# Sums of squares of the difference heads: two split passes with a low part from GpSimd, in place of one full-precision sum

## The chip, the cores and the metric

One core of a Trainium2 chip runs the whole program, a single launch. The metric is device time in microseconds (us) from one execution to the next of the same program, and a shorter time is better. Three runs of the kernel before are known, and one further execution that the hardware profiler recorded.

## What is computed

The program is a chain of two models on 512 tokens of width 1024, all in float32: one block with two kinds of attention, then four layers, each a mixer and a gated feed-forward network with a short convolution. The mixer is difference attention in layers 0 and 3, stick-breaking attention in layer 1 and sliding-window attention in layer 2. The change touches difference attention alone, and there only the norm of a head's output:

```python
def rmsnorm(x, g):
    xf = x.astype(jnp.float32)
    y = xf * lax.rsqrt(jnp.mean(xf * xf, axis=-1, keepdims=True) + EPS)
    return (y * g.astype(jnp.float32)).astype(x.dtype)

def diff_attention(h, w_qkv, lam, subln, rel_bias, lambda_init):
    ...
    def block(args):
        ...
        p = jax.nn.softmax(s, axis=-1)
        a = p[:, :, 0] - lam_full * p[:, :, 1]
        return jnp.einsum('bhqk,bkhe->bqhe', a.astype(v.dtype), v)

    o = lax.map(block, (q_blocks, jnp.arange(nb) * BLOCK))
    o = jnp.moveaxis(o, 0, 1).reshape(B, S, DA_HEADS, DA_V_DIM)
    o = rmsnorm(o, subln) * (1.0 - lambda_init)
    return o.reshape(B, S, DA_HEADS * DA_V_DIM)
```

There are 8 heads of 128 values each, and the mean of squares runs over the 128 values of a head, for each of the 512 tokens.

## The kernel before, in words

Each engine has a program of its own, written out by hand, and semaphores tie them together. A head's output lies with its 128 values on the partitions and the 512 tokens along the row, so a sum over the values is a product with a 128x128 matrix of ones, which also spreads the sum to all partitions.

**Products of the weights.** Weights come from memory in pieces of 128x2048. To multiply float32 data in single passes, each operand is split in two parts of the type fp32r: `whi` is the rounded weight (ScalarE, `split_hi`, L1162), `wlo` is the rest (GpSimd, four instructions of 512 columns a piece, L1113), and `three_passes` (L462) adds hi*hi, hi*lo and lo*hi. The data are split in the same way into `xh` and `xl`. Most of the kernel's TensorE time is spent in that one line.

**The mixer.** In `mix_diff` of TensorE (L909) the heads are staggered. Turn t of the loop works on head t: scores (L883), then their transposition (`turn`, L888). In the same turn it finishes head t-1: `pv` (L927) multiplies the weights of attention with the values, and `squares` (L933) sums the squares of the result, into the same PSUM bank `out`. Between these steps it fills in quanta of other work, the projections of later heads and, toward the end, the first part of the output product: `work.fill(n)` issues n quanta, `work.fill_to(n)` issues until n are done. A quantum is three passes of 512 columns where q and k are made, and six passes of 256 columns where v is made. `STARTS` says how many quanta must be done when a turn's scores begin, and three lines in the loop matter here:

```python
            work.fill(4 if last else 6)
            if t >= 1:
                squares(t - 1)
            work.fill_to(starts[t] + 20 if last else starts[t + 1] - 2)
            turn(t)
```

**What the other engines do in turn t.** VectorE (`mix_diff`, L1986) takes the scores from PSUM, adds the bias and their minimum (L2003), takes a projected unit, then copies the output of head t-1 to `od` (L2014), makes the low part of head t-2 (`ol`, L2018), the reciprocals (L2022, L2024), scales the second softmax (four instructions, `e1_scaled`, L2028), takes a projected unit (L1968), and combines the two softmaxes (four instructions, `normed`, L2033), which `turn` of TensorE waits for one by one. Then it reads the sum of squares of head t-1 (`ov`, L2040), waits for ScalarE's logarithm and exponential of it (L1452, L1454), scales the head (L2043), and takes the unit 3t+4 (L1968 for q and k, L1962 for v). Units 7, 13 and 19 are the k of heads 2, 4 and 6, and the scores of these heads wait for them.

ScalarE (`mix_diff`, L1419) copies the turned weights (`aT`, L1431), splits the head (L1435), takes the exponentials (L1416), squares `od` of head t-1 into `sq` (L1447), and then waits for `ov`. The table `HI_AT` says at which of three places of a turn it makes the high part of which piece: before the copy (place 0), after the exponentials (place 1) or after the square (place 2). In turns 1, 3 and 5 a piece stands at place 2, in turns 2, 4 and 6 one stands at place 1. GpSimd (`pool_program`) makes the low part of each piece as soon as its high part is there.

`var` is a buffer of the layer norms, which is free while a mixer runs.

## Time and profile before

| | |
|---|---|
| time, median of 3 runs | 2717.31 us (2715.97 to 2717.72) |
| time of the profiled execution | 2716.34 us |
| span of the profiled execution, first to last instruction | 2714.5 us |
| mean granted TensorE clock, share of full speed | 0.993 |
| TensorE (PE) busy | 2658.9 us, 98% of the span |
| TensorE weight loads (PEld) busy | 2129.7 us, 78% |
| VectorE (DVE) busy | 1460.9 us, 54% |
| GpSimd (POOL) busy | 1158.2 us, 43% |
| ScalarE (ACT) busy | 1117.7 us, 41% |

The difference between the profiled execution's time and its span, 1.8 us, lies before the first and after the last instruction. Busy shares are averages over the whole program. The first difference mixer lies at about 381 to 592 us of the span, the second at about 2111 to 2322 us. In the rows of the trace a matmul's own duration is longer than its share of the engine, since matmuls overlap in the array: the distance from one start to the next says what one costs. In the same way an instruction of VectorE is recorded from some 0.08 us before the one ahead of it ends.

### The profile page before, as it was taken

Reading aid. Unit: us, or ns where it says so; the run is one execution under the profiler, and the core shown is the slowest. Engines: PE = TensorE matmul, PEld = TensorE weight load, DVE = VectorE, ACT = ScalarE, POOL = GpSimd, SP = SyncE. Lnnn points to the kernel's source line nnn. Section 1 sums busy time; section 2 is a strip of 40 time slices with the busy share of each in tenths; the row PEclk is TensorE's granted clock in tenths of the full one; section 3 lists DMA queues with packets and bytes.
Section 4 is the critical chain, followed back from the end, with each engine's and each line's share of the span. In section 5 each row is a group of like instructions: output and inputs, shape, how many; then the busy total and the mean of one; then the engine's idle time right before and its main releaser. Section 6 shows DMA issues by size and latency. Waiting matters only on the chain.

```text
span 2714.5 us, 32020 instructions
## 1 busy us (share of the span) xinstructions
PE 2658.9 (98%) x12868; PEld 2129.7 (78%) x12868; DVE 1460.9 (54%) x2608; ACT 1117.7 (41%) x1509; POOL 1158.2 (43%) x876
## 2 busy tenths in 40 slices
PE   8998999999999999999999999999999999999997
PEld 7786687778888877778888886888888777888886
DVE  5797555557554135657554145575522565565522
ACT  4534644444333236654333236443333344443331
POOL 3353343235445532335444542254455332454452
PEclk9899999999999999999999999999999999999999
DMA  4125032222223221112223331222233222222332
GB/s 163 63 96 184 1 117 86 78 78 93 93 97 110 104 97 63 63 63 93 94 93 110 108 124 48 78 93 94 99 110 117 94 86 70 94 93 93 106 112 78
DMA packets 45605, 253.44 MB, mean 93 GB/s; under 512 B 4560, under 2 KB 9184, under 8 KB 17936
## 3 DMA queue, kind: packets, MB, share of 16 engines
q1 hardware_dynamic: 34656, 232.18, 24.4%
q10 hardware_dynamic: 10800, 19.20, 2.1%
q8 instruction: 102, 1.67, 0.2%
q14 instruction: 47, 0.39, 0.0%
HBM read 249.21 MB, written 10.55 MB: 96 GB/s over the span
## 4 chain that ended last, share of the span: by engine, by line
PE 92%; DVE 4%; ACT 2%; POOL 1%; issue 1%; DMA 0%; DVEq 0%; SPq 0%; ACTq 0%
PE ring L462 78%; PE ring L883 3%; PE turn L888 2%; PE turn L462 1%; PE out L927 1%; POOL wlo L1113 1%; PE ring L720 1%; PE ring L621 1%; PE out L736 1%; DVE sp L2065 1%; PE out L933 0%; DVE e L2033 0%; ACT whi L1162 0%; PE out L1015 0%; DVE z L2068 0%
## 5 line engine op out<-in xcount | busy, mean ns | idle before, releaser
L1113 POOL TENSOR_TENSOR wlo<-raw,whi 128x512 fp32r<-128x512 f32 x840 | 1124.0, 1369 | 1476.7 <-ACT whi L1162 1476.7
L462 PE MATMUL ring<-xh,whi 128*128 128x512 f32 x1888 | 753.2, 399 | 12.2 <-DVE xl L1616 8.5
L462 PE MATMUL ring<-xh,wlo 128*128 128x512 f32 x1888 | 736.8, 390 | 0.0
L462 PE MATMUL ring<-xl,whi 128*128 128x512 f32 x1888 | 736.3, 390 | 0.0
L1162 ACT ACTIVATE whi<-raw 128x2048 fp32r<-128x2048 f32 x215 | 411.2, 1913 | 432.7 <-DMA raw<-in_pieces 418.0
L462 PEld LDWEIGHTS ring<-xh,whi 128*128 128x128 f32 x1888 | 355.0, 188 | 117.5 <-issue 44.2
L462 PEld LDWEIGHTS ring<-xh,wlo 128*128 128x128 f32 x1888 | 354.9, 188 | 74.8
L462 PEld LDWEIGHTS ring<-xl,whi 128*128 128x128 f32 x1888 | 355.2, 188 | 72.4 <-issue 3.4
L2181 DVE SCALAR_TENSOR_TENSOR taps<-u,conv,taps 128x511 f32<-128x511 f32 (+1 forms) x344 | 296.9, 908 | 17.7 <-ACT taps L1558 15.7
L2195 DVE TENSOR_TENSOR u<-ring,r 128x512 f32<-128x512 f32 x168 | 114.3, 686 | 298.5 <-PE ring L462 298.5
L2169 DVE TENSOR_TENSOR h<-ring,h 128x512 f32<-128x512 f32 x72 | 49.5, 689 | 418.4 <-PE ring L809 376.1
L1558 ACT ACTIVATE taps<-u,conv 128x512 f32<-128x512 f32 x172 | 137.9, 808 | 303.5 <-DVE u L2195 303.5
L462 PE MATMUL ring<-hh,wlo 128*128 128x512 f32 x672 | 261.6, 389 | 0.0
L462 PE MATMUL ring<-hl,whi 128*128 128x512 f32 x672 | 261.6, 389 | 0.0
L462 PE MATMUL ring<-hh,whi 128*128 128x512 f32 x672 | 261.6, 389 | 0.0
L462 PE MATMUL ring<-whi,xh 128*128 128x256 f32 (+1 forms) x576 | 181.7, 315 | 0.7 <-POOL wlo L1113 0.7
L462 PE MATMUL ring<-wlo,xh 128*128 128x256 f32 (+1 forms) x576 | 173.8, 302 | 0.0
L462 PE MATMUL ring<-whi,xl 128*128 128x256 f32 (+1 forms) x576 | 173.6, 301 | 0.0
L462 PEld LDWEIGHTS ring<-hl,whi 128*128 128x128 f32 x672 | 126.2, 188 | 26.1
L462 PEld LDWEIGHTS ring<-hh,wlo 128*128 128x128 f32 x672 | 126.2, 188 | 26.1
L462 PEld LDWEIGHTS ring<-hh,whi 128*128 128x128 f32 x672 | 126.2, 188 | 26.1
L1561 ACT ACTIVATE taps<-taps 128x512 f32<-128x512 f32 x88 | 55.7, 633 | 173.7 <-DVE taps L2181 173.7
(282 smaller groups left out, 3410.9 us busy)
## 6 DMA issues: line engine op xcount, KB each, us to landing
raw<-in_pieces SPq DMA_DIRECT2D x215, 1024.0 KB, 4.7
toep<-diag_store ACTq DMA_DIRECT2D x16, 512.0 KB, 3.6
diag_store<-diag_row ACTq DMA_DIRECT2D x1, 5120.0 KB, 26.0
band_store<-band_row ACTq DMA_DIRECT2D x1, 3072.0 KB, 33.0
h<-in_x SPq DMA_DIRECT2D x4, 512.0 KB, 6.7
wbias<-band_store ACTq DMA_DIRECT2D x4, 512.0 KB, 7.3
result<-h SPq DMA_DIRECT2D x8, 256.0 KB, 2.1
raw<-in_pieces SPq DMA_DIRECT2D x4, 256.0 KB, 6.9
```

Source lines behind the costliest of these rows:

```text
L462: ins = pe.matmul(out, stationary, moving, start=first and n == 0, stop=last and n == 2)
L621: ins = pe.matmul(out, x[:, tok], weights[slot][:, w], start=i == 0 and weights is m.whi and x is passes[0][0], stop=i == len(tiles) - 1 a ...
L720: pe.matmul(bank(("score", p, j, i))[:, 0:n], q[:, i * P:(i + 1) * P], k[:, 0:n], start=True, stop=True).then_inc(m["unit_ready"], 1)
L883: pe.matmul(m.ring[2 + j][:, 0:n], qs[part, i * P:(i + 1) * P], ks[part, lo:lo + n], start=True, stop=True).then_inc(m["su_ready"], 1)
L888: ins = pe.transpose(m.turn[:, to:to + P], src[:, at:at + P], m.ident[:])
L1113: ins = pool.tensor_tensor(m.wlo[slot][:, part], m.raw[slot][:, part], m.whi[slot][:, part].bitcast(F32), ALU.subtract)
L1162: act.activation(m.whi[p % SLOTS][:], m.raw[p % SLOTS][:], ACT.Copy).then_inc(m["hi_done"], 1)
L1558: act.activation(taps[g][:], m.u[g][:], ACT.Identity, scale=cols[:, 4 * g + 2:4 * g + 3], bias=cols[:, 4 * g + 3:4 * g + 4]).then_inc(m["t ...
L1561: act.activation(taps[0][0:rows, :], taps[0][0:rows, :], ACT.Silu).then_inc(m["silu"], 1)
L2169: dve.tensor_tensor(m.h[:, k, :], ring(b, k)[:], m.h[:, k, :], ALU.add).then_inc(m["unit_taken"], 1)
L2181: dve.scalar_tensor_tensor(y[:, shift:S], m.u[g][:, 0:S - shift], cols[:, tap:tap + 1], y[:, shift:S], ALU.mult, ALU.add).then_inc(m[signa ...
L2195: dve.tensor_tensor(m.u[g][:], ring(b, 2 * t + g)[:], m.r[:], ALU.mult).then_inc(m["unit_taken"], 1)
```

## The change

For heads 0 to 6 of both difference mixers the sum of squares is taken in two passes over fp32r operands. ScalarE squares `od` twice: once in float32 into `sq`, as before, and once more, rounded to fp32r, into `osq_h` (in the place of `var`). GpSimd subtracts the one from the other and writes the rest as `osq_l` into the place of `sq`. TensorE multiplies both parts with `ones_r`, a copy of the ones as fp32r, and adds the two in PSUM. The last head of a mixer is summed as before. In TensorE's loop the sum stands four quanta later. GpSimd makes a head's low part after the low part of the last piece whose high part ScalarE makes ahead of that head's square. VectorE makes `ones_r` once, in the first stage.

```diff
--- before.py
+++ after.py
@@ -188,7 +188,7 @@
         heads = TILES if mixer == "diff" else 2 * TILES
         t.update({"turned": heads, "at_ready": heads})
         if mixer == "diff":
-            t.update(exped=64, rl_ready=8, c1_ready=8, e1_scaled=32, normed=32, o_taken=8, osq_ready=8, osum_done=8,
+            t.update(exped=64, rl_ready=8, c1_ready=8, e1_scaled=32, normed=32, o_taken=8, osq_ready=8, osqh_ready=7, osql_ready=7, osum_done=8,
                      ov_ready=8, oln_ready=8, ors_ready=8, on_ready=8)
         elif mixer == "stick":
             t.update(absed=16, expabs=16, lned=16, above_ready=16, scanned=64, arg_ready=16)
@@ -293,6 +293,7 @@
         self.cols = self.keep("cols", [P, N_COLS])
         self.ident = self.keep("ident", [P, P])
         self.ones = self.keep("ones", [P, P])
+        self.ones_r = self.keep("ones_r", [P, P], F32R)
         self.r = self.keep("r", [P, S])
         self.var = self.keep("var", [P, S])
         self.rtok = self.keep("rtok", [P, TT])
@@ -310,6 +311,9 @@
         sq_at = end - 4096
         self.sq = self.at("sq", [P, 2, S], sq_at)
         self.y = self.at("y", [P, S], sq_at)
+
+        self.osq_h = self.at("osq_h", [P, S], self.place["var"], F32R)
+        self.osq_l = self.at("osq_l", [P, 2, S], sq_at, F32R)
 
 
         consts = base + 49152
@@ -929,8 +933,15 @@
             ins.then_inc(m["pv_done"], 1)
 
         def squares(h):
-            pe.wait_ge(m["osq_ready"], b.at("osq_ready", h + 1))
-            pe.matmul(m.out[:], m.ones[:], m.sq[:, h % 2, :], start=True, stop=True).then_inc(m["osum_done"], 1)
+            if h == TILES - 1:
+                pe.wait_ge(m["osq_ready"], b.at("osq_ready", h + 1))
+                pe.matmul(m.out[:], m.ones[:], m.sq[:, h % 2, :], start=True, stop=True).then_inc(m["osum_done"], 1)
+                return
+
+            pe.wait_ge(m["osqh_ready"], b.at("osqh_ready", h + 1))
+            pe.matmul(m.out[:], m.ones_r[:], m.osq_h[:], start=True, stop=False)
+            pe.wait_ge(m["osql_ready"], b.at("osql_ready", h + 1))
+            pe.matmul(m.out[:], m.ones_r[:], m.osq_l[:, h % 2, :], start=False, stop=True).then_inc(m["osum_done"], 1)
         for t in range(TILES):
             work.fill_to(starts[t])
             pe.wait_ge(m["pu_taken"], b.at("pu_taken", K_UNIT[t] + 1))
@@ -943,7 +954,7 @@
                 work.fill(2)
             if t >= 1:
                 pv(t - 1)
-            work.fill(4 if last else 6)
+            work.fill(8 if last else 10)
             if t >= 1:
                 squares(t - 1)
             work.fill_to(starts[t] + 20 if last else starts[t + 1] - 2)
@@ -1099,12 +1110,27 @@
         for i in range(TT):
             row = m.e_1[p % 2][1][:, BLOCK_OFF[i]:BLOCK_OFF[i] + CAUSAL_W[i]]
             pool.tensor_scalar(row, row, m.rl[:, p % 2, 1, i:i + 1], None, ALU.mult).then_inc(m["normed_1"], 1)
+    def square_low(mb, h):
+
+
+        pool.wait_ge(m["osq_ready"], mb.at("osq_ready", h + 1))
+        pool.wait_ge(m["osqh_ready"], mb.at("osqh_ready", h + 1))
+        pool.tensor_tensor(m.osq_l[:, h % 2, :], m.sq[:, h % 2, :], m.osq_h[:].bitcast(F32),
+                           ALU.subtract).then_inc(m["osql_ready"], 1)
+
+    heads = {}
+    for name in st:
+        if name.startswith("mix") and MIXER[int(name[3:])] == "diff":
+            for h in range(TILES - 1):
+                last = max(j for j, where in HI_AT["diff"].items() if where <= (h + 1, 1))
+                heads.setdefault(st[name].at("piece", last), []).append((st[name], h))
     for p in range(1, n_pieces):
 
         if p == b.at("piece", 3):
             for pair in range(PAIRS):
                 normalise(pair)
         if p in by_vector:
+            assert p not in heads
             continue
         slot = p % SLOTS
         pool.wait_ge(m["hi_done"], p)
@@ -1113,6 +1139,8 @@
             ins = pool.tensor_tensor(m.wlo[slot][:, part], m.raw[slot][:, part], m.whi[slot][:, part].bitcast(F32),
                                      ALU.subtract)
         ins.then_inc(m["lo_done"], 1)
+        for mb, h in heads.get(p, ()):
+            square_low(mb, h)
 
 
 def sync_program(sp, m, d, ends, finish):
@@ -1445,6 +1473,10 @@
                 if h >= 2:
                     act.wait_ge(m["osum_done"], b.at("osum_done", h - 1))
                 act.activation(m.sq[:, h % 2, :], m.od[h % 3][:], ACT.Square).then_inc(m["osq_ready"], 1)
+                if h < TILES - 1:
+                    if h >= 1:
+                        act.wait_ge(m["osum_done"], b.at("osum_done", h))
+                    act.activation(m.osq_h[:], m.od[h % 3][:], ACT.Square).then_inc(m["osqh_ready"], 1)
             hi_at(b, "diff", t, 2)
             if 1 <= t < TILES + 1:
                 h = t - 1
@@ -1632,7 +1664,8 @@
         dve.wait_ge(m["unit_ready"], b.at("unit_ready", k + 1))
 
     def first(b):
-        dve.memset(m.ones[:], 1.0).then_inc(m["set_up"], 1)
+        chain(dve.memset(m.ones[:], 1.0))
+        dve.tensor_copy(m.ones_r[:], m.ones[:]).then_inc(m["set_up"], 1)
         for k in range(KT):
             if k % 2 == 0:
                 part = slice(256 * k, 256 * k + 512)
```

What moves can be seen in the order of the instructions. On TensorE, at the sum of head 0 in turn 1 (`xh` and `xl` are the data, `whi` and `wlo` the weights; the numbers in names count the buffers of the program). Before:

```order
L462 MATMUL ring<-xh,wlo_59 128x512
L933 MATMUL out<-sq,ones 128x512
L462 MATMUL ring<-xh,whi_56 128x512
L462 MATMUL ring<-xl,whi_56 128x512
L462 MATMUL ring<-xh,wlo_59 128x512
```

With the change:

```order
L466 MATMUL ring<-xh,whi_57 128x512
L466 MATMUL ring<-xl,whi_57 128x512
L466 MATMUL ring<-xh,wlo_60 128x512
L942 MATMUL out<-osq_h,ones_r 128x512
L944 MATMUL out<-osq_l,ones_r 128x512
L466 MATMUL ring<-xh,whi_57 128x512
```

The one sum has become two products, and they stand 12 matmuls later (row 1586 of TensorE's order, before row 1574), already among the matmuls of the next piece of weights. Where the quanta are those of v, as in turns 2, 4 and 6, four of them are 24 matmuls of 256 columns.

On GpSimd, from the low part of piece 4 to that of piece 7 (`wlo` is written over `raw`). Before:

```order
L1113 TENSOR_TENSOR wlo_60<-raw_54,whi_57 128x512 x4
L1113 TENSOR_TENSOR wlo_58<-raw_52,whi_55 128x512 x4
L1113 TENSOR_TENSOR wlo_59<-raw_53,whi_56 128x512 x4
L1113 TENSOR_TENSOR wlo_60<-raw_54,whi_57 128x512 x4
L1113 TENSOR_TENSOR wlo_58<-raw_52,whi_55 128x512 x4
```

With the change:

```order
L1139 TENSOR_TENSOR wlo_60<-raw_54,whi_57 128x512 x4
L1118 TENSOR_TENSOR osq_l<-sq,osq_h 128x512
L1139 TENSOR_TENSOR wlo_58<-raw_52,whi_55 128x512 x4
L1139 TENSOR_TENSOR wlo_59<-raw_53,whi_56 128x512 x4
L1118 TENSOR_TENSOR osq_l<-sq,osq_h 128x512
L1139 TENSOR_TENSOR wlo_60<-raw_54,whi_57 128x512 x4
L1118 TENSOR_TENSOR osq_l<-sq,osq_h 128x512
L1139 TENSOR_TENSOR wlo_58<-raw_52,whi_55 128x512 x4
```

The first `osq_l` is of head 0 (turn 1), and the low part of piece 5 now stands behind it. The second, of head 1 (turn 2), follows straight upon piece 6. The third is of head 2 (turn 3).

On ScalarE, behind the exponentials of turn 1. Before:

```order
L1403 DMA toep_190<-diag_store 128x2x512
L1447 ACTIVATE sq<-od_193 128x512
L1162 ACTIVATE whi_55<-raw_52 128x2048
L1452 ACTIVATE ov_191<-ov_191 128x512
L1454 ACTIVATE ov_191<-ov_191 128x512
```

With the change:

```order
L1431 DMA toep_193<-diag_store 128x2x512
L1475 ACTIVATE sq<-od_196 128x512
L1479 ACTIVATE osq_h<-od_196 128x512
L1190 ACTIVATE whi_55<-raw_52 128x2048
L1484 ACTIVATE ov_194<-ov_194 128x512
L1486 ACTIVATE ov_194<-ov_194 128x512
```

The second square stands ahead of the high part of piece 5.

## Rows read from the trace of the kernel before

**Rows 1.** The page's busy times, and the chain that ended last, by engine.
```profile
PE 2658.9 (98%) x12868; PEld 2129.7 (78%) x12868; DVE 1460.9 (54%) x2608; ACT 1117.7 (41%) x1509; POOL 1158.2 (43%) x876
...
PE 92%; DVE 4%; ACT 2%; POOL 1%; issue 1%; DMA 0%; DVEq 0%; SPq 0%; ACTq 0%
```
**Rows 2.** Timeline of PE, turns 1 and 4: start, length in us, engine, line, operation.
```profile
429.49 0.39 PE L462 MATMUL ring<-xl,whi 128*128 128x512 f32 x1
429.71 0.39 PE L462 MATMUL ring<-xh,wlo 128*128 128x512 f32 x1
...
432.52 0.49 PE L883 MATMUL ring<-kt,qt 64*128 64x128 f32 x4
...
496.44 0.28 PE L462 MATMUL ring<-whi,xl 128*128 128x256 f32 x1
496.56 1.02 PE L933 MATMUL out<-sq,ones 128*128 128x512 f32 x2
...
497.54 0.28 PE L462 MATMUL ring<-wlo,xh 128*128 128x256 f32 x1
```
**Rows 3.** Timeline of PE where turns 2, 3, 5 and 6 end.
```profile
454.34 0.36 PE L462 MATMUL ring<-whi,xh 128*128 128x256 f32 x1
...
481.07 0.49 PE L883 MATMUL ring<-kt,qt 64*128 64x128 f32 x4 [0.50 <-DVE kt L1968]
...
531.04 0.49 PE L883 MATMUL ring<-kt,qt 64*128 64x128 f32 x4
...
551.01 1.51 PE L888 MATMUL turn<-ident,e 128*128 128x128 f32 x10
552.28 0.37 PE L462 MATMUL ring<-whi,xh 128*128 128x256 f32 x1
```
**Rows 4.** Timeline of DVE, turn 2, and the last of L2033 in turn 6.
```profile
447.56 3.29 DVE L2028 TENSOR_SCALAR e<-e,c 128x128 f32<-128x128 f32 x4
450.77 0.68 DVE L1968 SCALAR_TENSOR_TENSOR kt<-ring,r 128x512 f32<-128x512 f32 x1
451.37 1.93 DVE L2033 SCALAR_TENSOR_TENSOR e<-e,rl,e 128x128 f32<-128x128 f32 x4
...
549.89 1.92 DVE L2033 SCALAR_TENSOR_TENSOR e<-e,rl,e 128x128 f32<-128x128 f32 x4
```
**Rows 5.** Timeline of DVE, turn 3, and where turn 5 ends.
```profile
470.03 1.28 DVE L2028 TENSOR_SCALAR e<-e,c 128x128 f32<-128x128 f32 x4
471.82 5.87 DVE L2033 SCALAR_TENSOR_TENSOR e<-e,rl,e 128x128 f32<-128x128 f32 x4
...
480.33 0.68 DVE L1968 SCALAR_TENSOR_TENSOR kt<-ring,r 128x512 f32<-128x512 f32 x1
...
530.18 0.68 DVE L1968 SCALAR_TENSOR_TENSOR kt<-ring,r 128x512 f32<-128x512 f32 x1
```
**Rows 6.** Timeline of POOL, turns 1 to 4.
```profile
423.61 6.04 POOL L1113 TENSOR_TENSOR wlo<-raw,whi 128x512 fp32r<-128x512 f32 x4 [14.20 <-ACT whi L1162]
...
444.49 5.48 POOL L1113 TENSOR_TENSOR wlo<-raw,whi 128x512 fp32r<-128x512 f32 x4 [14.84 <-ACT whi L1162]
...
471.58 5.57 POOL L1113 TENSOR_TENSOR wlo<-raw,whi 128x512 fp32r<-128x512 f32 x4 [9.46 <-ACT whi L1162]
...
493.01 5.48 POOL L1113 TENSOR_TENSOR wlo<-raw,whi 128x512 fp32r<-128x512 f32 x4 [15.86 <-ACT whi L1162]
```
**Rows 7.** Timeline of ACT, turns 1 and 3.
```profile
421.10 0.63 ACT L1447 ACTIVATE sq<-od 128x512 f32<-128x512 f32 x1 [2.96 <-DVE od L2014]
421.63 1.90 ACT L1162 ACTIVATE whi<-raw 128x2048 fp32r<-128x2048 f32 x1
...
478.33 0.63 ACT L1452 ACTIVATE ov<-ov 128x512 f32<-128x512 f32 x1 [6.83 <-DVE ov L2040]
```
**Rows 8.** Timeline of DVE, turn 1.
```profile
421.47 1.28 DVE L2028 TENSOR_SCALAR e<-e,c 128x128 f32<-128x128 f32 x4
423.27 3.99 DVE L2033 SCALAR_TENSOR_TENSOR e<-e,rl,e 128x128 f32<-128x128 f32 x4
```

## The prediction, made before the change was run

> **What bounds the kernel now.** I read the page first. TensorE is busy for 98% of the span and holds 92% of the chain that ended last [rows 1], so time that leaves TensorE shows in the total, unless another engine takes it back, and time that another engine gains or loses counts only where TensorE waits for it. Those places had to be found in the timelines, because inside the two difference mixers TensorE has little slack beside VectorE. Rows 3 show three such places a mixer. In turn 3 the scores of head 4 wait 0.50 us for `kt`. In turn 5 the scores of head 6 start at 531.04, right behind the `kt` of rows 5, which ends at 530.18 + 0.68 = 530.86. In turn 6 the transposition takes 1.27 us to the next matmul (551.01 to 552.28): it waits in its middle for the last `normed`. So I had to price the change on both engines.
>
> **The gain on TensorE.** In turn 4 the last narrow pass before the sum starts at 496.44, the second behind it at 497.54 [rows 2]. Two narrow steps of 0.12 us would take 0.24 of that, so the sum costs 1.10 - 0.24 = 0.86 us. (Its recorded 1.02 us contains overlap.) The two passes that replace it have the form of L462's, of 512 columns, two of which start 0.22 us apart, at 429.49 and 429.71 [rows 2]; other pairs of them lie 0.23 apart, the rows being rounded. I take 0.23 each, 0.46 for both. That is 0.40 us less per head, and 14 heads give 5.6 us if nothing else moves. Making `ones_r` in the first stage is one short operation of VectorE while the first data are still on their way, so it costs nothing (0.7 us if that cover were gone, by a 512-column operation of VectorE [rows 4]).
>
> **ScalarE.** A second square costs one more step of 0.53 us, the distance from `sq` to the next instruction [rows 7]. ScalarE then waits for `ov` anyway (6.83 us idle in turn 3 [rows 7]), which hides it. Not hidden is that the high part of a piece, where one follows the square (turns 1, 3, 5), comes 0.53 us later, and GpSimd's low part with it.
>
> **GpSimd, and what it does to VectorE.** This is the term that decides. GpSimd's new instruction has the size of one of its four per piece: 5.48 us for four, two of which VectorE stretches [rows 6], so near 1.3 us each. Rows 4 and 5 show what such an instruction does to VectorE where VectorE reads and writes SBUF alone. The four L2028 take 1.28 us in turn 3, with GpSimd idle, and 3.29 us in turn 2, with two of GpSimd's instructions beside them: 1.0 us for each. The four L2033 take 1.93 us in turn 2 and 5.87 us in turn 3, beside four: again 1.0 us for each. The two take turns, instruction by instruction. `qt` and `kt`, which read PSUM, take 0.68 us either way. I take 1.0 us for a hit; the bounds are 0 (GpSimd's instruction meets only PSUM readers) and 1.3 us (all of it).
>
> The Trainium skill, page "SBUF — State Buffer", section "Who interferes with whom", says that the pair of ports shared by VectorE and GpSimd is an exclusive lock, held for a whole instruction, and that the loser blocks fully. By that a hit could cost all of GpSimd's instruction, 1.3 us in place of 1.0, and the sum below would be 1.2 us higher. The rows show 1.0, since VectorE's own time partly overlaps the wait, and I stay with them.
>
> **Turn by turn**, with the shift of TensorE against before at the start of the next scores (negative is earlier). All numbers are of mixer 0; mixer 3 repeats its rows.
>
> - Turn 1 (head 0). GpSimd's low part can start when the second square ends: 421.63 + 0.63, and 0.08 to wake (as from 421.63 + 1.90 to 423.61 [rows 6, 7]), 422.34. The four L2028 end at 422.75 [rows 8], and the fourth, of 512 columns, takes somewhat under 0.5 us, so it starts near 422.27. I take VectorE to be first. Then GpSimd starts at 422.75, L2033 loses some 0.5 us, and ends at 427.8 in place of 423.27 + 3.99 = 427.26 [rows 8]. The scores of head 2 (432.52) have room for that, so the shift is -0.40.
> - Turn 2 (head 1). GpSimd goes on from 444.49 + 5.48 = 449.97 [rows 6] straight into the low part and hits the third L2028 (+1.0). `normed` ends at 453.30 [rows 4] - 0.40 + 1.0 = 453.90. In turn 6 the next matmul comes 0.47 us after the last `normed` (549.89 + 1.92 = 551.81 [rows 4], then 552.28 [rows 3]), so here at 454.37, against 454.34 [rows 3]. Shift +0.03: the gain is lost.
> - Turn 3 (head 2). The low part hits L2028 (+1.0), but L2033 starts inside GpSimd's work on the piece in any case, and its end is set by that, which is 0.53 later. `kt` ends at 481.01 [rows 5] + 0.03 + 0.53 = 481.57, the scores start 0.06 later at 481.63 against 481.07. Shift +0.56.
> - Turn 4 (head 3). VectorE loses 1.0 but is early enough. TensorE comes to the second pass at 496.56 + 24 * 0.12 + 0.23 = 499.67; the low part is there at 493.01 + 5.48 + 1.28 + 0.08 = 499.85 [rows 2, 6]. A wait of 0.18, and some 0.1 to start again. Shift +0.56 - 0.40 + 0.3 = +0.46.
> - Turn 5 (head 4). As turn 3, `kt` ends at 530.86 + 0.46 + 0.53 = 531.85, scores at 531.91 against 531.04. Shift +0.87.
> - Turn 6 (head 5). The transposition already waits for `normed`, which is another 1.0 later. Shift +1.87.
> - Turn 7 (head 6). VectorE has room; TensorE keeps its 0.40. Shift +1.47.
>
> So each mixer ends 1.5 us later, and the two together 2.9 us. Against the profiled execution's own 2716.34 us that is 2719.2 us. It lies 1.0 us below the median of the runs, so the forecast is 2717.31 + 2.9 = 2720.2 us: 0.1% slower, which a measurement of this kernel can hardly tell from no change (about 0.2%, 5.4 us, is what it can tell).
>
> **Rival 1, slower: GpSimd is first in turn 1.** The two starts in turn 1 lie 0.07 us apart, and no row settles who wins such a meeting. If GpSimd gets in before the fourth L2028, that instruction ends near 423.8, `qt` near 424.4, and by then GpSimd has begun the piece (423.61 + 0.53 = 424.14). L2033 then runs as in turn 3, 5.87 us from 424.3 to 430.2, not to 427.26. From there to the end of `kt` turn 3 needs 481.01 - 477.69 = 3.3 us [rows 5], so `kt` is ready at 433.5, and the scores of head 2 start 1.0 us late, not 0.4 early. That is 1.45 us a mixer on top of everything above: +5.8 us, 2723.1 us. For it speaks that the gap is so small; against it that VectorE's instruction is recorded first. The page named above says, in the same section, that whoever starts first has the lock for the whole instruction. By the recorded starts this favours my forecast, and by the real end of the instruction ahead (0.08 us later than the record) it favours this rival.
>
> **Rival 2, faster: the collisions fall into slack.** If the low part meets only PSUM readers or idle time and nothing else is late, TensorE still cannot be earlier at the scores of head 4 or in the transposition of turn 6, since `kt` and `normed` wait for VectorE there. The gain of turns 3 and 6 is lost, and of turn 5 about 0.3. What stays is near 0.40 * 4 + 0.1 = 1.7 us a mixer: -3.4 us, 2713.9 us. Against it speaks that in turns 2, 4 and 6 GpSimd's fifth instruction follows the fourth without a pause, beside VectorE's L2028.
>
> **Rival 3, the whole gain.** If the waits of rows 3 shift along with the scores that begin their turn and VectorE is never the limit, all 5.6 us arrive: 2711.7 us. The 0.50 us wait in rows 3 speaks against it.
>
> **How the numbers follow.** I give the forecast 0.45, with another 0.07 for a course between it and rival 2, rival 1 0.28, rival 2 0.12, rival 3 with whatever else would make it faster 0.08. The range has to reach rival 2 on one side and rival 1 with a full price of hits (+1.2 us) on the other: 2713.2 to 2724.4 us. Faster by over 0.2% (below 2711.9) is rival 3 alone, 0.10 with the tail of rival 2. Slower by over 0.2% (above 2722.7) is rival 1 and the dear end of the forecast, 0.30. Within 0.2% stays 0.60.
>
> **What would show each step.** Two fp32r products in place of L933, 0.23 us apart or with a short wait before the second in turns 4 and 6. The four L2028 at 4.3 us in turns 2, 4 and 6 and at 2.3 us in turns 3, 5 and 7, in place of 3.29 and 1.28. The four L2033 near 4.5 us in turn 1 (forecast) or 5.9 us (rival 1). A wait for `kt` before the scores of head 4 near 1.4 us and a new one before those of head 6; a transposition in turn 6 that takes over 2 us. The forecast is wrong if L2028 keeps its length, if the scores of head 2 wait for `kt`, or if the waits before the second product are longer than a few tenths.

## The result, and the profile after

The changed kernel takes 2720.35 us (median of 22 runs, 2717.58 to 2722.81), the kernel before 2715.64 us (median of 22 runs beside them, 2714.39 to 2717.72): 4.7 us more. The ratio is 1.0016, with a 95% interval of 1.001 to 1.0022. The profiled execution of the changed kernel took 2721.88 us, its span 2720.1 us.

| start of the scores of turn, us | 0 | 1 | 2 | 3 | 4 | 5 | 6 | 7 |
|---|---|---|---|---|---|---|---|---|
| before | 386.45 | 408.05 | 432.52 | 455.95 | 481.07 | 505.78 | 531.04 | 553.88 |
| after | 388.47 | 410.07 | 434.16 | 458.35 | 484.13 | 508.76 | 534.55 | 558.43 |
| shift, less that of turn 0 | 0 | 0.00 | -0.38 | +0.38 | +1.04 | +0.96 | +1.49 | +2.53 |

The row "shift" is what the scores of a turn come later than before, less the same difference at turn 0. At the copy of the last head's output the shift is +2.16 us. The second difference mixer repeats this within 0.02 us and ends at +2.15. So the two mixers lose 4.3 us, which is most of the 4.7 us. Turn 0 of the first mixer starts 2.02 us late in this execution. No sum stands ahead of it; the last section comes back to that.

The page of the changed kernel, busy times and the chain by engine:

```profile
PE 2658.3 (98%) x12868; PEld 2129.2 (78%) x12868; DVE 1479.2 (54%) x2609; ACT 1124.7 (41%) x1523; POOL 1177.3 (43%) x890
...
PE 89%; DVE 6%; ACT 2%; POOL 1%; issue 1%; DMA 0%; SPq 0%; DVEq 0%; ACTq 0%
```

Against [rows 1], TensorE's busy time is 0.6 us less and its share of the chain fell from 92% to 89%, while VectorE's rose from 4% to 6%. VectorE is busy 18.3 us longer, though it got one instruction more, of 0.23 us: the rest is time in which its instructions are recorded as running and wait. Not all of that is the change's. By stretches, VectorE's busy time in each of the two mixers grew from 120.7 to 128.0 us, 7.3 us for seven instructions of GpSimd or 1.05 us each, while 3.6 us more stand ahead of the first mixer, where no sum is taken. The share of a busy engine says nothing of this; only a comparison of the same line does.

TensorE in turn 1 of the changed kernel (start, length in us, engine, line):

```profile
428.80 0.40 PE L466 MATMUL ring<-xh,wlo 128*128 128x512 f32 x1
429.03 0.39 PE L942 MATMUL out<-osq_h,ones_r 128*128 128x512 f32 x1
429.26 0.40 PE L944 MATMUL out<-osq_l,ones_r 128*128 128x512 f32 x1
429.50 0.39 PE L466 MATMUL ring<-xh,whi 128*128 128x512 f32 x1
```

Both passes cost 0.47 us, from 429.03 to 429.50, as priced from [rows 2]. The gain on TensorE is there. What takes it back are the waits at the end of the turns:

```profile
454.20 0.38 PE L466 MATMUL ring<-whi,xh 128*128 128x256 f32 x1 [0.71 <-DVE kt L2001]
...
484.13 0.49 PE L887 MATMUL ring<-kt,qt 64*128 64x128 f32 x4 [1.26 <-DVE kt L2001]
...
502.53 0.40 PE L942 MATMUL out<-osq_h,ones_r 128*128 128x512 f32 x1
502.93 0.50 PE L944 MATMUL out<-osq_l,ones_r 128*128 128x512 f32 x1
503.27 0.28 PE L466 MATMUL ring<-whi,xh 128*128 128x256 f32 x1
...
534.55 0.49 PE L887 MATMUL ring<-kt,qt 64*128 64x128 f32 x4 [0.87 <-DVE kt L2001]
...
554.92 2.16 PE L892 MATMUL turn<-ident,e 128*128 128x128 f32 x10 [0.36 <-DVE e L2066]
556.83 0.36 PE L466 MATMUL ring<-whi,xh 128*128 128x256 f32 x1
```

Beside [rows 3]: the wait for `kt` before the scores of head 4 has grown from 0.50 to 1.26 us, the one before head 6 is new, and the transposition of turn 6 takes 1.91 us to the next matmul, not 1.27, after a wait of 0.36. New as well, and not foreseen, is the wait at 454.20. In turn 4 the sum takes 0.74 us (502.53 to 503.27), 0.27 us more than in turn 1: 0.17 us before the second pass, which waits for the low part, and 0.10 us behind it.

VectorE in turns 1, 2 and 3 of the changed kernel:

```profile
423.49 1.28 DVE L2061 TENSOR_SCALAR e<-e,c 128x128 f32<-128x128 f32 x4
...
425.28 4.46 DVE L2066 SCALAR_TENSOR_TENSOR e<-e,rl,e 128x128 f32<-128x128 f32 x4
...
449.19 4.35 DVE L2061 TENSOR_SCALAR e<-e,c 128x128 f32<-128x128 f32 x4
453.47 0.68 DVE L2001 SCALAR_TENSOR_TENSOR kt<-ring,r 128x512 f32<-128x512 f32 x1
454.07 1.93 DVE L2066 SCALAR_TENSOR_TENSOR e<-e,rl,e 128x128 f32<-128x128 f32 x4
...
472.43 2.33 DVE L2061 TENSOR_SCALAR e<-e,c 128x128 f32<-128x128 f32 x4
...
475.28 5.48 DVE L2066 SCALAR_TENSOR_TENSOR e<-e,rl,e 128x128 f32<-128x128 f32 x4
```

and GpSimd beside it:

```profile
424.42 1.51 POOL L1118 TENSOR_TENSOR osq_l<-sq,osq_h 128x512 fp32r<-128x512 f32 x1 [12.96 <-ACT osq_h L1479]
...
446.13 5.50 POOL L1139 TENSOR_TENSOR wlo<-raw,whi 128x512 fp32r<-128x512 f32 x4 [13.98 <-ACT whi L1190]
451.60 1.33 POOL L1118 TENSOR_TENSOR osq_l<-sq,osq_h 128x512 fp32r<-128x512 f32 x1
...
472.75 1.40 POOL L1118 TENSOR_TENSOR osq_l<-sq,osq_h 128x512 fp32r<-128x512 f32 x1 [7.92 <-ACT osq_h L1479]
474.49 5.72 POOL L1139 TENSOR_TENSOR wlo<-raw,whi 128x512 fp32r<-128x512 f32 x4 [0.35 <-ACT whi L1190]
```

The four instructions that scale the second softmax (L2028 before, L2061 now) went from 3.29 to 4.35 us in turn 2, with `osq_l` straight behind the piece, and from 1.28 to 2.33 in turn 3 [rows 4, 5]. In turns 4 and 6 they take 4.36 us (3.29 before), in turns 5 and 7 2.33 and 2.32. In turn 1 they kept 1.28 us [rows 8]: VectorE was first there, and GpSimd's instruction is stretched to 1.51 us. From here on VectorE's two groups are called by their lines in the kernel before, L2028 and L2033, whatever the line of a row is (here L2061 and L2066).

### The profile page after: what moved, and what is told of

It is laid out like the page before. It is cut to its first block, busy times and chain, and to the rows that moved or that the text cites. A ratio compares the mean times of both kernels' runs of the same rounds, so it can differ in the third digit from the quotient of the medians.

```text
span 2720.1 us, 32063 instructions
## 1 busy us (share of the span) xinstructions
PE 2658.3 (98%) x12868; PEld 2129.2 (78%) x12868; DVE 1479.2 (54%) x2609; ACT 1124.7 (41%) x1523; POOL 1177.3 (43%) x890
## 3 DMA queue, kind: packets, MB, share of 16 engines
q8 instruction: 102, 1.67, 0.2%
## 4 chain that ended last, share of the span: by engine, by line
PE 89%; DVE 6%; ACT 2%; POOL 1%; issue 1%; DMA 0%; SPq 0%; DVEq 0%; ACTq 0%
PE ring L466 76%; PE ring L887 3%; PE turn L892 2%; PE turn L466 1%; PE out L931 1%; POOL wlo L1139 1%; PE ring L724 1%; PE ring L625 1%; DVE e L2061 1%; DVE e L2066 1%; PE out L740 1%; DVE sp L2098 1%; ACT whi L1190 0%; PE out L1026 0%; DVE z L2101 0%
## 5 line engine op out<-in xcount | busy, mean ns | idle before, releaser
L466 PEld LDWEIGHTS ring<-whi,xh 128*128 128x128 f32 x576 | 110.3, 192 | 21.6 <-issue 12.4
```

The costliest lines, as they stand in the source:

```text
L466: ins = pe.matmul(out, stationary, moving, start=first and n == 0, stop=last and n == 2)
```

## The experiments

Two theories stood against each other. By mine, the loss comes from GpSimd's new instruction, which holds up VectorE where both work in SBUF, and TensorE feels it only where it waits for VectorE. By the other, it comes from TensorE's own waiting for the low part, from the later place of the sums, or from what was added around them. All times are medians beside runs of the kernel before on the same chip. Shifts are read as in the table above, in the first mixer, for the scores of turns 2 to 7; the number given for the end is that at the copy of head 7's output. The diffs show the lines that matter, and "..." marks what is left out.

**The ones alone.** Kernel before, with

```diff
+        self.ones_r = self.keep("ones_r", [P, P], F32R)
-        dve.memset(m.ones[:], 1.0).then_inc(m["set_up"], 1)
+        chain(dve.memset(m.ones[:], 1.0))
+        dve.tensor_copy(m.ones_r[:], m.ones[:]).then_inc(m["set_up"], 1)
```

> The kernel before with nothing added but ones_r: its 512 bytes and the one cast of VectorE in the first stage. Mine: no change, within 0.5 us of before, and the 2 us that the changed kernel's profile lost at 250 us of the span (a stretch at the lower TensorE clock) come and go from one execution to the next whatever the kernel. Rival: the shifted start of the program brings that stretch about, then the times fall into two groups some 2.5 us apart and the median is 1 to 2 us above before.

Measured: 2716.5 us against 2715.89, ratio 1.0002 (0.9993 to 1.0011). No shift in either mixer exceeds 0.04 us. The median is 0.6 us up, where I had allowed 0.5, but the interval holds no change, and the times don't fall into the rival's groups 2.5 us apart. The placement in SBUF and the cast cost nothing that can be measured.

**GpSimd's instruction without the gain.** The changed kernel with TensorE's sums as before:

```diff
-            pe.matmul(m.out[:], m.ones_r[:], m.osq_h[:], start=True, stop=False)
...
-            pe.matmul(m.out[:], m.ones_r[:], m.osq_l[:, h % 2, :], start=False, stop=True).then_inc(m["osum_done"], 1)
+            pe.matmul(m.out[:], m.ones[:], m.sq[:, h % 2, :], start=True, stop=True).then_inc(m["osum_done"], 1)
...
-            work.fill(8 if last else 10)
+            work.fill(4 if last else 6)
...
-        pool.tensor_tensor(m.osq_l[:, h % 2, :], m.sq[:, h % 2, :], m.osq_h[:].bitcast(F32),
+        pool.tensor_tensor(m.osq_h[:], m.sq[:, h % 2, :], m.osq_h[:].bitcast(F32),
...
                 if h >= 2:
                     act.wait_ge(m["osum_done"], b.at("osum_done", h - 1))
+                    act.wait_ge(m["osql_ready"], b.at("osql_ready", h - 1))
...
-                        act.wait_ge(m["osum_done"], b.at("osum_done", h))
+                        act.wait_ge(m["osql_ready"], b.at("osql_ready", h))
```

ScalarE's squares now also wait for GpSimd's instruction of an earlier head, since that one reads and overwrites their buffers.

> TensorE's sums stay as before (full precision, old place). ScalarE squares twice, and GpSimd subtracts, in place, onto osq_h, which nobody reads. Mine (the loss comes from GpSimd's instruction beside VectorE): slower than before by 4.0 to 5.0 us, L2028's four at 4.3 us in turns 2, 4, 6 and 2.3 us in turns 3, 5, 7; the scores of head 4 and head 6 wait for kt, the transposition of turn 6 for normed. Rival (the loss comes from TensorE waiting for the low part, or from the later place of the sum): within 1 us of before.

Measured: 2722.37 us against 2715.89, ratio 1.0024 (1.0015 to 1.0033), 6.5 us slower. The shifts at the scores of turns 2 to 7 are 0.00, +0.75, +1.39, +1.42, +1.93, +2.97, and +2.93 at the end. Each mixer loses 2.9 us though TensorE does just what it did. The loss is VectorE's, and it is more than I expected; the wait for the low part and the later place of the sum are no part of it. Set beside the changed kernel this says something more. Turns 2, 3, 5 and 6 add +0.75, +0.64, +0.51 and +1.04 here, and +0.76, +0.66, +0.53 and +1.04 there: in these four turns VectorE sets the end, and TensorE's gain is worth nothing at all. It is kept in turns 1 and 7, and some 0.1 us of it in turn 4.

**The gain without GpSimd's instruction.** The changed kernel, with

```diff
-            pe.wait_ge(m["osql_ready"], b.at("osql_ready", h + 1))
-            pe.matmul(m.out[:], m.ones_r[:], m.osq_l[:, h % 2, :], start=False, stop=True).then_inc(m["osum_done"], 1)
+            pe.matmul(m.out[:], m.ones_r[:], m.osq_h[:], start=False, stop=True).then_inc(m["osum_done"], 1)
...
-        for mb, h in heads.get(p, ()):
-            square_low(mb, h)
```

> The change without GpSimd's instruction: both passes multiply osq_h (so the sums are twice the rounded squares' sum, and the low part is left out). Mine: TensorE keeps 0.40 us a head except in turns 3 and 6, and loses about 0.5 us in turns 3 and 5 to the later piece; 1 to 2 us faster than before, 6 us faster than the change. L2028 back at 3.29 and 1.28 us. Rival (the passes or their place cost the time): still 3 us or more slower than before.

Measured: 2711.52 us against 2715.89, ratio 0.9984 (0.9975 to 0.9993), 4.4 us faster. Shifts: -0.41, -0.69, -1.69, -2.05, -1.63, -1.63, at the end -2.00. So the passes and their place gain, and GpSimd's seven instructions, with TensorE's waits for them, turn -2.00 into +2.16 us a mixer. The gain is larger than expected, and turn 3 says why. VectorE and GpSimd in turn 3 of this kernel:

```profile
468.96 1.27 DVE L2058 TENSOR_SCALAR e<-e,c 128x128 f32<-128x128 f32 x4
...
470.75 4.00 DVE L2063 SCALAR_TENSOR_TENSOR e<-e,rl,e 128x128 f32<-128x128 f32 x4
```

```profile
471.01 6.13 POOL L1138 TENSOR_TENSOR wlo<-raw,whi 128x512 fp32r<-128x512 f32 x4 [9.64 <-ACT whi L1187]
```

Here the piece's low part starts 0.26 us after VectorE's L2033, not 0.24 us before it as in [rows 5, 6], and the four take 4.00 us in place of 5.87: only two of them still meet an instruction of GpSimd. The rows of the last three, one by one:

```profile
471.01 0.48 DVE L2063 SCALAR_TENSOR_TENSOR e<-e,rl,e 128x256 f32<-128x256 f32 x1
471.40 1.65 DVE L2063 SCALAR_TENSOR_TENSOR e<-e,rl,e 128x384 f32<-128x384 f32 x1
472.97 1.78 DVE L2063 SCALAR_TENSOR_TENSOR e<-e,rl,e 128x512 f32<-128x512 f32 x1
```

Before, the same three take 1.51, 1.64 and 1.77 us.

**The second square alone.** The kernel of "GpSimd's instruction without the gain" without its `square_low` and without the waits for it, so that nothing but ScalarE's square (and the ones) is added.

> The kernel before with ScalarE's second square alone, which nobody reads. Mine: the pieces of turns 1, 3 and 5 come 0.53 us later, GpSimd's work on them too, and VectorE ends its L2033 0.5 us later in turns 3 and 5: shifts of +0.5 us at the scores of head 4 and +0.9 us at those of head 6, in all +1.9 us for the two mixers. Rival (ScalarE has idle time, so its square is hidden): 0.

Measured: 2716.15 us against 2715.89, ratio 1.0002 (0.9992 to 1.0012). The shifts are 0.00, 0.00, -0.57, -0.54, -0.15 and -0.19, at the end -0.22: a little faster within the mixers, where I expected 1 us slower in each. VectorE and GpSimd in turn 3:

```profile
474.77 3.99 DVE L2057 SCALAR_TENSOR_TENSOR e<-e,rl,e 128x128 f32<-128x128 f32 x4
```

```profile
475.04 6.12 POOL L1132 TENSOR_TENSOR wlo<-raw,whi 128x512 fp32r<-128x512 f32 x4 [9.96 <-ACT whi L1181]
```

The piece comes half a microsecond later, as priced, but that lets VectorE start first, and its four instructions lose 1.9 us less. Turn 5 goes the other way: the piece comes first there in both kernels, by 0.81 us before and by 0.28 us now, and L2033 takes 5.85 us in place of 5.30.

**Heads 0 and 6 alone.** `SPLIT = (0, 6)` in place of `h < TILES - 1` in the programs of TensorE, GpSimd and ScalarE, the other heads as before the change:

```diff
-            if h == TILES - 1:
+            if h not in SPLIT:
...
-            work.fill(8 if last else 10)
+            split = t - 1 in SPLIT
+            work.fill((8 if split else 4) if last else (10 if split else 6))
...
-                if h < TILES - 1:
+                if h in SPLIT:
```

> The change for heads 0 and 6 of a mixer alone, the others as before (sum in full precision, two quanta places as before, no second square, no low part). Mine: these are the two heads whose turns have room on VectorE, so each keeps its 0.40 us: 0.8 us a mixer, 1.6 us faster than before. Rival (a gain on TensorE in turn 1 is lost at the wait for kt in turn 3 whatever comes between): 0.8 us faster.

Measured: 2714.78 us against 2716.22, ratio 0.9995 (0.9986 to 1.0003); the interval holds no change. The trace tells more: shifts of -0.39 at each turn from 2 to 6, -0.40 at turn 7, -0.75 at the end, in both mixers. Each of the two heads keeps its 0.4 us, and what turn 1 gains passes through the wait for `kt` in turn 3, as VectorE moved with it.

**One pass over rounded squares.** No second square, no low part, the sum in its old place; the low part of the squares is left out.

```diff
-            pe.matmul(m.out[:], m.ones_r[:], m.osq_h[:], start=True, stop=False)
-            pe.wait_ge(m["osql_ready"], b.at("osql_ready", h + 1))
-            pe.matmul(m.out[:], m.ones_r[:], m.osq_l[:, h % 2, :], start=False, stop=True).then_inc(m["osum_done"], 1)
+            pe.matmul(m.out[:], m.ones_r[:], m.osq_l[:, h % 2, :], start=True, stop=True).then_inc(m["osum_done"], 1)
...
-            work.fill(8 if last else 10)
+            work.fill(4 if last else 6)
...
-                act.activation(m.sq[:, h % 2, :], m.od[h % 3][:], ACT.Square).then_inc(m["osq_ready"], 1)
+                dst = m.osq_l if h < TILES - 1 else m.sq
+                act.activation(dst[:, h % 2, :], m.od[h % 3][:], ACT.Square).then_inc(m["osq_ready"], 1)
```

> One pass over squares that ScalarE rounds to fp32r, in the sum's old place, for heads 0 to 6; no second square, no work of GpSimd. The low part of the squares is left out. Mine: 0.63 us less on TensorE per head, of which turns 3 and 6 and part of turn 5 give nothing back, since VectorE sets their ends: 4 to 5.5 us faster than before. Rival (TensorE alone sets the time): 14 heads by 0.63 us, 8.8 us faster.

Measured: 2712.04 us against 2716.22, ratio 0.9986 (0.9977 to 0.9995), 4.2 us faster. Shifts: -0.66, -0.94, -0.92, -1.55, -1.67, -1.69, at the end -2.40. Turn 3 and turn 6 add nothing to the gain (-0.94 to -0.92, -1.67 to -1.69): VectorE sets their ends.

**The low part in two halves.**

```diff
-        pool.tensor_tensor(m.osq_l[:, h % 2, :], m.sq[:, h % 2, :], m.osq_h[:].bitcast(F32),
+        pool.tensor_tensor(m.osq_l[:, h % 2, 0:256], m.sq[:, h % 2, 0:256], m.osq_h[:, 0:256].bitcast(F32),
+                           ALU.subtract)
+        pool.tensor_tensor(m.osq_l[:, h % 2, 256:512], m.sq[:, h % 2, 256:512], m.osq_h[:, 256:512].bitcast(F32),
                            ALU.subtract).then_inc(m["osql_ready"], 1)
```

> The change with GpSimd's low part in two instructions of 256 columns. Mine: VectorE's loss goes with the length of the instruction that it meets, less the part that overlaps, so two short ones cost about 0.7 us in place of one of 1.0 us, and turns 2 and 6 each end 0.3 us earlier: 1 us faster than the change. Rival (the loss is the whole time that GpSimd works): the same as the change. Second rival (a fixed cost for each of GpSimd's instructions): 2 us in place of 1 in turns 2, 4 and 6, some 4 us slower than the change.

Measured: 2720.71 us against 2716.22, ratio 1.0015 (1.0006 to 1.0024), as slow as the change. VectorE and GpSimd in turn 2:

```profile
449.81 4.28 DVE L2063 TENSOR_SCALAR e<-e,c 128x128 f32<-128x128 f32 x4
...
452.32 0.89 DVE L2063 TENSOR_SCALAR e<-e,c 128x384 f32<-128x384 f32 x1
453.13 0.96 DVE L2063 TENSOR_SCALAR e<-e,c 128x512 f32<-128x512 f32 x1
```

```profile
452.21 0.78 POOL L1118 TENSOR_TENSOR osq_l<-sq,osq_h 128x256 fp32r<-128x256 f32 x1
452.95 0.85 POOL L1120 TENSOR_TENSOR osq_l<-sq,osq_h 128x256 fp32r<-128x256 f32 x1
```

4.28 us in place of 4.35: two short instructions cost VectorE nearly what one long one does. The first rival holds. The first row is all four of L2028, the next two are its third and fourth. They take 0.41 and 0.48 us in the kernel before, so each loses 0.48 us to one short instruction; in the changed kernel the third alone loses 1.04 us to the long one. A meeting's price goes with the length of GpSimd's instruction, as I had said, but less than I had said of it overlaps, so that two halves come to the price of the whole.

**The low part on VectorE.**

```diff
-        for mb, h in heads.get(p, ()):
-            square_low(mb, h)
...
                 take_qk_v(b, 3 * t + 3, -0.125)
+                if t >= 1:
+                    h = t - 1
+                    dve.wait_ge(m["osqh_ready"], b.at("osqh_ready", h + 1))
+                    dve.tensor_tensor(m.osq_l[:, h % 2, :], m.sq[:, h % 2, :], m.osq_h[:].bitcast(F32),
+                                      ALU.subtract).then_inc(m["osql_ready"], 1)
                 for i in range(TT):
                     dve.wait_ge(m["e1_scaled"], b.at("e1_scaled", TT * t + i + 1))
```

> The change with the low part made by VectorE, between its projected unit and L2033. Mine: 0.68 us of VectorE in place of 1.0 us lost to GpSimd's instruction, so turns 2 and 6 each end 0.3 us earlier and turns 3 and 5 stay: 1.3 us faster than the change, still 3 us slower than before. Rival (it collides with the piece's low part and waits for one of GpSimd's instructions too): 1.0 us more than that in turn 3 and 5, no faster than the change.

Measured: 2722.11 us against 2716.22, ratio 1.0021 (1.0011 to 1.0031), slower still. The shifts are -0.37, +0.17, +0.97, +1.67, +2.75 and +3.35, at the end +3.00. VectorE saves the collision in turn 2 (L2028 at 3.31 us) but comes to the low part too late for TensorE, which waits between the two passes:

```profile
452.82 0.50 PE L944 MATMUL out<-osq_l,ones_r 128*128 128x512 f32 x1 [0.67 <-DVE osq_l L2065]
```

It waits 0.78 us there in turns 4 and 6. Neither my expectation nor the rival named this wait. The rival's outcome came true, no faster than the change, and its collision shows in turn 5, where VectorE's `osq_l` takes 1.57 us (0.67 in turn 2).

**Three pieces moved out of VectorE's way.** If the meeting of the two engines is what costs, it can be taken away without touching the sums. The line moves the high parts of pieces 5, 8 and 11 to the start of the next turn. One line is added to the kernel before:

```diff
+HI_AT["diff"] = {**HI_AT["diff"], 5: (2, 0), 8: (4, 0), 11: (6, 0)}
```

> The kernel before with the high parts of pieces 5, 8 and 11 made at the start of the next turn (place 0 of turns 2, 4, 6) in place of behind the square, so that GpSimd's low parts of them fall beside the scores, where VectorE reads PSUM. The squares as before. Mine: L2033 at 1.93 us in turns 1, 3 and 5, no wait for kt before the scores of head 4, which gives back its 0.5 us a mixer: 1 us faster than before. Rival (the pieces come too late for TensorE, or ScalarE's later aT holds up pv): slower.

Measured: 2715.35 us against 2715.75, ratio 0.9998 (0.9989 to 1.0007). Turn 3 on VectorE, GpSimd and TensorE:

```profile
471.88 1.93 DVE L2034 SCALAR_TENSOR_TENSOR e<-e,rl,e 128x128 f32<-128x128 f32 x4
...
477.48 0.69 DVE L1969 SCALAR_TENSOR_TENSOR kt<-ring,r 128x512 f32<-128x512 f32 x1 [0.96 <-PE ring L463]
```

```profile
477.62 5.02 POOL L1114 TENSOR_TENSOR wlo<-raw,whi 128x512 fp32r<-128x512 f32 x4 [15.45 <-ACT whi L1163]
```

```profile
480.54 0.49 PE L884 MATMUL ring<-kt,qt 64*128 64x128 f32 x4
```

L2033 is down from 5.87 to 1.93 us, VectorE now waits for TensorE before `kt`, and the 0.50 us wait for `kt` is gone (shift -0.57 from turn 4 on, -0.56 and -0.52 at the ends). VectorE gained 4 us in that turn and TensorE half a microsecond, since only that much was waited for. The times agree with 1 us but cannot tell it from nothing.

**The same with the change:** the same line, added to the changed kernel.

> The change with the same three pieces moved. Mine: what is lost in turns 3 and 5 to kt comes back and TensorE keeps its 0.40 us there; the losses in turn 2 (kt, for a PSUM bank) and turn 6 (normed) stay, about 0.8 us each: 1 to 1.5 us faster than before, 6 us faster than the change. Rival (every one of GpSimd's instructions costs, wherever the pieces stand): at most 2 us faster than the change.

Measured: 2715.93 us against 2715.75, ratio 1.0 (0.9991 to 1.0009). Shifts: -0.39, +0.36, -0.62, -0.68, -1.07, +0.01, at the end -0.35. The move takes 2.5 us a mixer off the change, somewhat less than the 3 us foreseen, and the kernel is not measurably faster than before. Turns 3 and 5 now keep their gain. Turn 2 (+0.75) and turn 6 (+1.08) keep their losses: there the low part still follows a piece. Turn 4, where the second pass still waits for the low part, adds only -0.06.

**The move, and the split for heads 0, 2, 4 and 6 alone.** The line above and `SPLIT = (0, 2, 4, 6)`.

> The three pieces moved, and the split sum for heads 0, 2, 4 and 6 alone, whose low parts do not follow upon a piece's. Mine: 0.40 us a head for four heads and the 0.5 us of the kt wait, 2.0 us a mixer: 4 us faster than before. Rival (turns 2, 4, 6 lose on VectorE what the turns before them gain): 1 us faster.

Measured: 2712.78 us against 2715.75, ratio 0.9989 (0.998 to 0.9998), 3.0 us faster. Shifts: -0.39, -0.39, -1.37, -1.34, -1.75, -1.75, at the end -2.11. This version computes the whole sum and beats both kernels, though its interval comes close to no change. I had expected 4 us. The two mixers are in fact 4.2 us shorter in the profiled execution; where the other 1.2 us went, or whether it is scatter, no run shows.

**The move, and one pass over rounded squares.** The low part is left out again.

> The three pieces moved, and one pass over squares rounded to fp32r for heads 0 to 6 (their low part is left out). Mine: 0.63 us a head but for turn 6 and some 0.3 us in turn 2, and the 0.5 us of kt: 3.5 to 4 us a mixer, 7 to 8 us faster than before. Rival (the waits for VectorE in turns 3 and 5 have other causes than GpSimd's pieces): 5 us faster, as without the move.

Measured: 2707.67 us against 2715.75, ratio 0.9971 (0.9959 to 0.9982), 8.1 us faster, at the end of the mixers -4.11 and -4.10. It is the fastest of all, at the price of sums of squares that carry only the fp32r part.

## Why the prediction was right, and where it was off

The forecast was 2720.2 us and the measurement 2720.35, well within the range. That the two agree within 0.2 us is luck: the median of before that I started from (2717.31, three runs) came out 1.7 us lower with 22 runs, the difference was 4.7 us where I had forecast 2.9, and the two errors cancel. The measured 0.16% is inside the band that I called no change, though with 22 runs the interval of the ratio leaves out 1. The ends of my range lay 0.7 us below rival 2's sum and 0.1 us above that of rival 1 with the dear hits; no row stood for that.

Step by step, shift added by each turn:

| turn | 1 | 2 | 3 | 4 | 5 | 6 | 7 | sum |
|---|---|---|---|---|---|---|---|---|
| predicted | -0.40 | +0.43 | +0.53 | -0.10 | +0.41 | +1.00 | -0.40 | +1.47 |
| measured | -0.38 | +0.76 | +0.66 | -0.08 | +0.53 | +1.04 | -0.37 | +2.16 |

**The gain on TensorE** (0.40 us a head) was right: 0.47 us for both passes, -0.38 and -0.37 in the turns with room. The experiment without a low part shows most of it in turn 4 (-0.36), but only -0.28 in turn 2, for a reason given below.

**GpSimd's price** of 1.0 us was right: L2028 gained 1.06 us in turn 2 and 1.05 in turn 3. In turn 2 it is the third of the four, before and after:

```profile
450.05 0.41 DVE L2028 TENSOR_SCALAR e<-e,c 128x384 f32<-128x384 f32 x1
```

```profile
451.70 1.45 DVE L2061 TENSOR_SCALAR e<-e,c 128x384 f32<-128x384 f32 x1
```

The Trainium skill, "SBUF — State Buffer", section "Who interferes with whom", has the loser blocked for the whole of the other's instruction. The lengths of L2028 would have grown by 1.3 us by that; they grew by 1.05. The trace agrees in kind and not in size: alone, GpSimd's four instructions take 5.02 us and VectorE's four 1.93 (both in the kernel with three pieces moved), 6.95 in all, and in turn 3 of the kernel before both groups are done in 6.11 us, from 471.58 to 477.69. So some 0.2 us of a meeting overlap. Which part of an instruction it is that can overlap, no run shows.

**Turn 1** went as forecast: VectorE first (four at 1.28 us, then 4.46 us for L2033, where I had 4.5 and rival 1 had 5.9). It was close: the fourth L2028 starts at 424.29 and GpSimd's instruction at 424.42.

```profile
424.29 0.48 DVE L2061 TENSOR_SCALAR e<-e,c 128x512 f32<-128x512 f32 x1
```

The Trainium skill's rule, in the same section, that the first to start has the lock agrees with the recorded starts there.

**Turn 2 is the step that failed.** I took the transposition to be the place where TensorE meets VectorE, and priced the turn at +0.03 us of shift; it came to +0.38. TensorE meets VectorE before that, at the second unit of the piece of v, whose quanta need the PSUM bank that VectorE empties with `kt` (the unit's wait on `pu_taken`). `kt` ended at 453.47 + 0.68 = 454.15, and TensorE went on at 454.20, after 0.71 us. The transposition behind it did not wait (1.25 us, as before). In the kernel before, the same matmul, the twelfth ahead of the transposition, is this one:

```profile
451.89 0.28 PE L462 MATMUL ring<-whi,xh 128*128 128x256 f32 x1
```

`kt` ended at 450.77 + 0.68 = 451.45 there [rows 4], so the bank was free only 0.44 us in time and no row of before shows the wait. That is little more than TensorE's own gain, and so this bank also takes part of the gain where GpSimd adds nothing: without the low part turn 2 adds -0.28 in place of -0.40, and with one pass -0.29 in place of -0.65. The lesson is plain: I asked who waits for the last instruction of the delayed row, and not who waits for those in its middle.

**Turns 3 and 5** were priced by the piece's delay of 0.53 us and cost 0.66 and 0.53. The size was nearly right, the reason only in part. In the changed kernel VectorE does end behind the piece, which in turn 3 starts 0.51 us later in its turn and takes 5.72 us in place of 5.57: that is the 0.66. But I said that this holds in any case; the second square's delay by itself, however, makes turn 3 faster (-0.57), since VectorE then starts ahead of GpSimd and escapes two of the four meetings. In the changed kernel the low part's hit on L2028 pushes VectorE back behind the start of the piece (by 0.79 us), and L2033 takes 5.48 us, so all four are met again. Without the low part turn 3 adds -1.00, with it +0.66: one instruction of 1.3 us costs 1.7 us there, more than my upper bound for a hit.

**Turns 4 and 6** were right: a wait and restart of 0.27 us at the second pass where I had 0.3, and a transposition of turn 6 that comes 1.04 us later where I had 1.0.

**Rival 2 and rival 3** fell with the experiment without TensorE's gain: the collisions do not fall into slack. But the experiment without the low part beat rival 2's price (-2.00 a mixer, not -1.7), for the reason just given.

## What to carry to other kernels

Work that is moved to an idle GpSimd is not free when VectorE works in SBUF at that time: count its instructions, put each beside what VectorE does then, and price it at the length by which the same VectorE line differs in the trace with and without GpSimd. Then look for every one who waits for VectorE's later instructions, the middle ones too, since a bank or a buffer that was free in time before may not be any more. Before adding to such a meeting, try to move it: placing three existing pieces beside PSUM work was one line, and it made the split worth having for heads 2 and 4 beside heads 0 and 6, which kept their gain without it.

## What was not expected of the hardware

**Half a microsecond's delay can save two.** The same four instructions of VectorE took 5.87 us when GpSimd's piece began 0.24 us before them and 3.99 us when it began 0.27 us after. GpSimd's four took 5.57 us in the first case and 6.12 in the second. Who is first decided the whole row that followed, so a delay on a third engine (here ScalarE's square) can be a gain.

**A stretch at the lower clock moves the time by more than the change's own terms.** At 250 to 255 us of the span both kernels are at the same place of the program. Windows of the kernel before and of the changed one (length; PE, PEld, DVE, ACT and POOL busy, each with its count of instructions; granted clock; busy share of the DMA engines, GB/s):

```profile
250.00:255.00 5.00, 5.00 (x29) 3.61 (x28) 4.12 (x19) 4.47 (x16) 3.05 (x3) 1.00 0.79 300
```

```profile
250.00:255.00 5.00, 5.00 (x12) 2.83 (x11) 2.85 (x12) 3.34 (x12) 3.37 (x3) 0.66 0.93 352
```

The granted clock was 1.00 in the first and 0.66 in the second, a part of it at 1.2 GHz in place of 2.4. TensorE had been busy for 1.93 of the 5 us ahead of it, in both kernels. Together with it the first mixer starts 2.0 us later. Other kernels of this study (the one without a low part, for one) show such a stretch near there as well, and the kernel with the ones alone doesn't, so I take it for a matter of the single execution. The kernel with the second square alone speaks for that: in its profiled execution the clock was 0.51 there and the first mixer starts 2.94 us late, and that execution is the longest of its eight (2718.56 us, the shortest 2714.77). The 22 times of the changed kernel lie in two groups of eleven (2717.58 to 2719.47 and 2721.23 to 2722.81), which may be this; the mean clock was 0.993 or 0.994 in the first and 0.992 or 0.993 in the second. The shorter eleven have a median 3.7 us above that of the shorter eleven of before, the longer eleven 5.1 us above that of the longer. Whether the change makes the stretch more frequent stays open, and the difference of the medians (4.7 us) may hold some tenths of it beyond the mixers' 4.3.
